# A two-block transformer kernel: last two early modulation panels awaited singly, the low part of weight panel 0 on GpSimd, panel 1 rounded after the tiles, and the last two dilated turns issued one unit ahead

## The reference, cut to what matters

```python
c_act = jax.nn.silu(c)
mod = c_act @ w_ada[l] + b_ada[l]                 # 1024 x 6144
sh1, sc1, gt1, sh2, sc2, gt2 = split(mod, 6)
h = rms_norm(x, g_norm1[l]) * (1.0 + sc1) + sh1
proj = h @ w_in[l]                                # q, k, v of both attentions, gates
...
o_a = neighbourhood_attention(qa, ka, va, rpb[l]) # 8 heads
...
for g, (win, dil) in enumerate(DIL_CONFIGS):      # 3 groups of 4 heads
    o_g, lse_g = dilated_window_attention(qb[:, :, sl], kb[:, :, sl], vb[:, :, sl], win, dil)
wts = jax.nn.softmax(jnp.stack(lses, axis=0), axis=0)
o_b = einsum('gbsh,gbshd->bshd', wts, stack(outs))
merged = gate_a * (o_a @ w_proj_a[l]) + gate_b * (o_b @ w_proj_b[l])
x = x + gt1 * (merged @ w_o[l])
```

## Time and profile before

| | us |
|---|---|
| runs, median of 3 | 2263.01 (2259.01 to 2263.64) |
| the profiled execution, its own time | 2256.2 |
| its span | 2254.4 |
| PE busy | 2141.8 (95%) |
| PE weight loads busy | 1874.1 (83%) |
| DVE busy | 1330.2 (59%) |
| ACT busy | 1137.2 (50%) |
| POOL busy | 61.4 (3%) |

### The profile page before, as it was taken

One profiled execution on the slowest core, in us unless ns is written; L12 is line 12 of the kernel. 1 busy time (PEld: TensorE's weight loads), 2 busy tenths in 40 slices (PEclk: granted clock), 3 DMA queues, 4 the chain that ended last, 5 costly groups with the idle time before them and its releaser, 6 DMA issues. The chain is left out here.

```text
span 2254.4 us, 40901 instructions
## 1 busy us (share of the span) xinstructions
PE 2141.8 (95%) x15620; PEld 1874.1 (83%) x15620; DVE 1330.2 (59%) x1845; ACT 1137.2 (50%) x1673; POOL 61.4 (3%) x74
## 2 busy tenths in 40 slices
PE   6999889999999999989999999999999997999998
PEld 5787778887888988888998887887997897998887
DVE  3446375556556985565655555555896564756555
ACT  3453644445445555654445445444556563535444
POOL 0000000000000010000000000000002000000000
PEclk8999999999999999999999999999999999999999
DMA  9663245554553443421455554554444321355553
GB/s 398 235 240 111 75 157 187 186 186 170 188 187 145 184 157 127 166 79 58 151 186 194 186 186 170 189 187 167 155 180 150 140 104 41 131 187 186 187 186 121
DMA packets 53328, 373.24 MB, mean 166 GB/s; under 512 B 6304, under 2 KB 6304, under 8 KB 9280
## 3 DMA queue, kind: packets, MB, share of 16 engines
q1 hardware_dynamic: 47664, 342.00, 41.9%
q0 software_dynamic: 5520, 29.23, 3.6%
HBM read 370.10 MB, written 1.11 MB: 165 GB/s over the span
## 5 line engine op out<-in xcount | busy, mean ns | idle before, releaser
L1419 ACT ACTIVATE HI<-ring 128x1024 fp32r<-128x1024 f32 x606 | 625.1, 1054 | 762.8 <-PE banks L536 397.6
L1962 DVE TENSOR_TENSOR LO<-ring,HI 128x1024 fp32r<-128x1024 f32 x318 | 389.1, 1226 | 369.2 <-ACT HI L1419 368.9
L1968 DVE TENSOR_TENSOR LO<-ring,HI 128x2048 fp32r<-128x2048 f32 x139 | 318.5, 2291 | 255.1 <-ACT HI L1419 249.7
L500 PE MATMUL banks<-UH,HI 128*128 128x256 f32 x1392 | 406.4, 292 | 5.3 <-DVE LO L1968 5.3
L501 PE MATMUL banks<-UL,HI 128*128 128x256 f32 x1392 | 396.2, 285 | 0.0
L502 PE MATMUL banks<-UH,LO 128*128 128x256 f32 x1392 | 396.1, 285 | 0.0
L534 PE MATMUL banks<-HI,UH 128*128 128x512 f32 x896 | 349.4, 390 | 7.1 <-DVE LO L1968 4.9
L536 PE MATMUL banks<-HI,UL 128*128 128x512 f32 x896 | 348.7, 389 | 0.0
L535 PE MATMUL banks<-LO,UH 128*128 128x512 f32 x896 | 348.7, 389 | 0.0
L500 PEld LDWEIGHTS banks<-UH,HI 128*128 128x128 f32 x1392 | 269.3, 193 | 22.6 <-issue 15.9
L501 PEld LDWEIGHTS banks<-UL,HI 128*128 128x128 f32 x1392 | 269.5, 194 | 1.4 <-issue 1.2
(11 more groups left out here) (326 smaller groups left out, 3089.9 us busy)
## 6 DMA issues: line engine op xcount, KB each, us to landing
ring<-in_w_stream SPq DMA_DIRECT2D x315, 1024.0 KB, 4.8
ARENA<-in_ada_stream POOLq DMA_DIRECT2D x16, 1024.0 KB, 5.1
ARENA<-in_ada_stream SPq DMA_DIRECT2D x8, 1024.0 KB, 14.8
GRMS<-cum_rows POOLq DMA_DIRECT2D x16, 256.0 KB, 3.5
ARENA<-in_na_bias POOLq DMA_DIRECT2D x2, 1024.0 KB, 13.2
RMS<-cum_rows POOLq DMA_DIRECT2D x8, 256.0 KB, 3.4
RSTD<-cum_rows POOLq DMA_DIRECT2D x8, 256.0 KB, 3.7
ARENA<-in_ropes POOLq DMA_DIRECT2D x1, 1088.0 KB, 18.7
```

What stands on the lines that cost most here:

```text
L500: nc.tensor.matmul(out, lh, rh, start=start, stop=False, **kw)
L1419: nc.scalar.activation(HI[:, q % PARTS, at], ring[:, q % RING, at], ACT.Copy).then_inc(hi_ready, 1)
L1962: nc.vector.tensor_tensor(LO[:, q % PARTS, at], ring[:, q % RING, at], HI[:, q % PARTS, at].bitcast(F32), ALU.subtract).then_inc(lo_ready, 1)
L1968: nc.vector.tensor_tensor(LO[:, q % PARTS, :], ring[:, q % RING, :], HI[:, q % PARTS, :].bitcast(F32), ALU.subtract).then_inc(lo_ready, 2)
```

## The change

```diff
+ADA1_GROUP = (0, 0, 0, 0, 1, 1, 2, 3)
...
+TURN_AHEAD = TURNS - 2
...
+        def turn_bank(u):
+
+            return 0 if u >= TURN_AHEAD and u % 2 == TURN_AHEAD % 2 else 2
...
             for i in range(ADA_FIRST):
-                sp.dma_start(ADA1[:, i, :], ada_stream[i]).then_inc(ada1_loaded[i // 2], 16)
+                sp.dma_start(ADA1[:, i, :], ada_stream[i]).then_inc(ada1_loaded[ADA1_GROUP[i]], 16)
...
         def _(pool):
 
+            for h in range(2):
+                pool.wait_ge(hi_ready, h + 1)
+                at = slice(h * PANEL // 2, (h + 1) * PANEL // 2)
+                nc.gpsimd.tensor_tensor(LO[:, 0, at], ring[:, 0, at], HI[:, 0, at].bitcast(F32),
+                                        ALU.subtract).then_inc(lo_ready, 1)
             pool.wait_ge(ada_rows_done, ADA_FIRST)
...
                 if n < ADA_FIRST:
-                    pe.wait_ge(ada1_loaded[n // 2], 32)
+                    pe.wait_ge(ada1_loaded[ADA1_GROUP[n]], 16 * ADA1_GROUP.count(ADA1_GROUP[n]))
...
-                if u >= 1:
+                if u == TURN_AHEAD:
+                    pe.wait_ge(scored, TURNS)
+                    pe.wait_ge(pt_copied, u - 1)
+                elif u > TURN_AHEAD:
+                    pe.wait_ge(pt_copied, u - 1)
+                elif u >= 1:
                     pe.wait_ge(pt_copied, u)
                 for e in range(2):
                     for k in range(2):
-                        mm = nc.tensor.transpose(bank[2][:, (2 * e + k) * P:(2 * e + k + 1) * P],
+                        mm = nc.tensor.transpose(bank[turn_bank(u)][:, (2 * e + k) * P:(2 * e + k + 1) * P],
...
                     k = DIL_GROUPS * d + g
-                    turn(NA_UNITS + k)
+                    if NA_UNITS + k < TURN_AHEAD:
+                        turn(NA_UNITS + k)
+                    if TURN_AHEAD <= NA_UNITS + k + 1 < TURNS:
+                        turn(NA_UNITS + k + 1)
...
             root(0)
             split(0)
+            fill_high(u_ready, lambda k: 2 * k + 2)
             split(1)
-            fill_high(u_ready, lambda k: 2 * k + 2)
...
-                nc.scalar.activation(PT[:, u % 2, :], bank[2][:, :], ACT.Copy).then_inc(pt_copied, 1)
+                nc.scalar.activation(PT[:, u % 2, :], bank[turn_bank(u)][:, :], ACT.Copy).then_inc(pt_copied, 1)
...
             ada_take(0)
-            split(0)
...
             scaled_fill(0, FILL_B1_NORM1, GS[:, 0:8], shift1, FIRST_BANKS)
+            dve.wait_ge(lo_ready, 2)
             split(1)
```

## The result

The changed kernel takes 2266.86 us (median of 22 runs), the kernel before 2259.05 us on the same chips (22 runs); the ratio is 1.0033, 95% interval 1.0025 to 1.0041: slower by 7.4 us by that ratio, clear of the noise. The forecast was a loss of 2.8 us that would mostly read as none (2265.8 us, counted from a median of 2263.01 that more runs brought to 2259.05), with a chance of 0.27 for a clear one. The sign and the place were right; the size was not. That 2266.86 lies so near 2265.8 is luck: the base fell by 4.0 us, and the loss came out 4.6 us larger than forecast.

A forecast was written before the change was run, and what follows sets the result against it. PE, busy 95% of the span, was taken as the bound, so only its waits could be saved. +2.9 us at panel 10 and -0.1 at the last dilated units gave +2.8 on the median 2263.0: 2265.8 us, range 2260 to 2270.5.

The forecast's parts named there:

- Edit 1: Start: modulation panels 6 and 7 awaited singly; sum copied at 30.6 instead of 32.4, taking 1.8 us off the path.
- Edit 2: Start: low part of panel 0 made on GpSimd instead of DVE; first product at 37.3, 0.5 us earlier.
- Edit 3: Start, ACT's order: tiles no longer wait for panel 1's rounding; its LO at 45.2, wanted at 46.9.
- a twentieth of 30 us: DMA engines, 32 to 62: closable gaps, put at 1.3 us, lowering the 4.7 us delay; panel 10 lands at 61.5 earliest.
- The rival of the one-column gains: Start: one-column gains also wait for GpSimd's second half, PE starts at 39.3; +1.4 if panel 10 is in time; chance 0.05.
- What GpSimd was to do meanwhile: Start: five DMA issues 4.7 us later, SP's refill late, engines dry about 34.5 to 39; panel 10 late, +2.9 us.
- The forecast landing of 63.5: Modulation panel 10's load: lands at 63.5 instead of 58.1, the middle of bounds 61.5 and 65.4.
- The clock rival: At panel 10: PE idles 3.4 us and its clock drops too; +4.3 to +7 us, 2269 at the middle; chance 0.25.
- Edit 4: Last dilated units: turns one unit ahead, but ACT's order sets unit 19's copy; -0.1 us, bounds 0 and -0.7.

The follow-up runs named there:

- e7: Kernel before with only the semaphores of the modulation panels regrouped for single waits; ratio 1.0002 to the kernel before.
- e6: Kernel before with LO of panel 0 on GpSimd and tiles rounded ahead of panel 1, without single waits or turns ahead; ratio 1.0032.
- e2: Changed kernel with the two bias loads and the rotary tables issued behind modulation panel 10; ratio 1.0006 to the kernel before.
- e1: Changed kernel with GpSimd's five DMA issues put ahead of its two subtractions; ratio 0.9999 to the kernel before.
- e5: Kernel before with one added wait: GpSimd's DMA issues wait until the first tiles are rounded; ratio 1.0020.
- e9: Kernel before with two added waits: GpSimd's DMA issues and SP's first ring refill wait until the first tiles are rounded; ratio 1.0032.
- e11: Kernel before with the last turns one unit ahead and ACT's copy of unit 19 ahead of the spread rows' second copies; ratio 0.9985.

## Why the prediction was right, and where its size failed

- **Edit 1** (panel 7 alone, copy at 30.6): right in kind. The copy came at 30.07, because the clock had stayed full through the modulation in this execution; that it has no effect while DVE waits for ACT's halves is shown by e7.
- **Edit 2, the first product at 37.3, set by GpSimd's LO:** right (37.63, 37.06, 37.32 in the changed kernel, e6 and e2, each released by GpSimd). In the changed kernel's own trace the gains came before GpSimd began (31.43), so they did not wait; in e6 they did, as described. LO decided either way.
- **Edit 3:** right. LO of panel 1 was started at 41.78 and done at 44.07 (forecast 45.2), and PE went on to panel 1 at 46.93 without a wait. Two small slips did no harm: UL takes 0.69 us on a free DVE, not 0.55, and a twentieth of 30 us is 1.5, not 1.3.
- **The rival of the one-column gains:** they would have waited for GpSimd's second half. They took 0.14 us at the change from the first half to the second (e6, and e2 the same), and the rival, with its chance of 0.05, did not come. The Trainium skill, page "VectorE: DVE Perf Modes", section "Mode 2×_2P — use both read ports for one tensor", asks for an even outermost dimension of more than one element, or an odd one that is equal on both sides; a one-column operation has none, so these rows hardly test it. What speaks against it is the earlier trace rows: 407 ns for 256 columns, where 1.1 ns a column is the rate of the two-source subtraction.
- **What GpSimd was to do meanwhile:** the place, the cause (five issues at 37.5 instead of 32.6, SP's refill at 37.8, engines dry from about 34.5 to 38.5) and the victim (panel 10) were right, and e1, e5 and e9 show the cause by taking it away and by making it alone. The forecast landing of 63.5 with a bound of 65.4 failed: 66.5. The step that failed is the conversion of a late start into a late landing. I carried 4.7 us through the queue one to one and added at most one weight panel. But what is lost in a gap is bytes, 1.71 MB, and panel 10 gets them back only at the share of GpSimd's queue. From 60 to 64 that queue moved 0.98 MB (row below), 0.25 MB a microsecond; its 1.70 MB of deficit at 58 (4.96 against 6.66 MB since 34) take 6.9 us at that rate, where the engines' whole 408 GB/s would make them up in 4.2. Measured, panel 10 landed 8.4 us later than before, so 1.5 us are left over. The bytes suggest panel 11 for them: it was issued at 54.70, into the same queue. The six loads up to panel 10 are 6.36 MB. When panel 10 landed, the queue had moved 6.69 MB since its first issue before, and 7.23 in the changed kernel, so about 0.5 MB more of panel 11 had gone in between; no run separates the two panels. The Trainium skill, page "DMA: Bandwidth & Descriptors", section "Queues, rings and completion order", says that each DMA engine takes turns between its queues packet by packet. The trace shows both queues served side by side, but not in even turns: 134 packets and 59% of the engines' time for this queue, 82 packets and 40% for SP's.
- **The clock rival** (0.25) is what happened: the 5.73 us wait was followed by half clock, worth 1.28 us at once, which the forecast's sum had at nothing. Its price of +4.3 to +7 ends just short of the measured 7.4, because the wait was longer than the 3.4 us that I had priced. The prediction had two waits to go by, 3.8 us with half clock behind it and 2.5 us without. The length of the wait alone does not sort them: in e5 the clock fell within 1.7 us of the end of a wait of only 1.86 us, and in e2 it stayed at 1.00 for 1.2 us after a wait of 3.71 us and then stood at 0.55 from 72.5 to 75.
- **Edit 4, -0.1:** too small as a term (-1.5 to -1.8 to the projection), nearly right in the end (about -0.3). That nearness is luck: the half-clock stretch moves instead of going, which I had not named. That ACT's order holds unit 19's copy back was right, and e11 shows it.
- Scatter between single executions (2.9 below and 3.4 above the medians) is nearly as large as the whole effect; the landmarks in the trace are steadier.

The rows for GpSimd's queue (q0) and SP's (q1) in the changed kernel, 60 to 64 us (columns: packets, MB, share of the 16 engines' time):

```profile
q0 software_dynamic: 134, 0.98, 59.3%
q1 hardware_dynamic: 82, 0.67, 40.1%
```

## What to carry to other kernels

Before work is put at the head of a queue, list what that queue was to issue, and everything else that waits for the same result: here two DMA queues stood behind one subtraction, and the engines ran dry in a stretch in which they had no slack. Count such a gap in bytes, divide by the rate that the late queue gets, and compare with the slack of the last load in it; for panel 10 this gives 6.9 of the 8.4 us. And when PE's waits are shortened, look whether a half-clock stretch disappears or only moves.

## What the runs showed of the hardware that was not expected

- A DVE operation with two SBUF inputs and 8 columns took 1.18 us and (in e2) 2.12 us beside a GpSimd subtraction of 2.34 us per half. Whether DVE gets in between two subtractions in a row differs: in the changed kernel it did after the first half (UL took 1.41 us from 33.96), and the second half then took 2.79 us instead of 2.35; in e1 DVE stood from 34.02 to 38.41, through both, and both took 2.34 to 2.36. No run here tells why.
- In one trace of each kernel, the half-clock stretch at the last dilated units was in the same place in all five kernels without the turns ahead, and at the projection in all seven with them alone, though the traces differ elsewhere in when the clock falls. The two with the copy moved as well show none there.
